# A decoder step on one core: bank copies in the up projection's first pair, and prompt keys kept on chip between two sparse attentions

## What is computed

```python
def swiglu(x, w_gu, w_down):
    gate, up = jnp.split(x @ w_gu, 2, axis=-1)
    return (jax.nn.silu(gate) * up) @ w_down

def indexer_scores(iq, iw, ik):                       # which keys a query may see
    dots = jax.nn.relu(jnp.einsum('bqhd,bsd->bqhs', iq, ik).astype(F32))
    return jnp.einsum('bqhs,bqh->bqs', dots, iw.astype(F32))
# dsa_prompt: per block of 128 queries, scores -> top 256 keys -> softmax(q k^T) v over them
# dsa_sample: the same for 8 queries of a sequence over 2,048 cached keys and 8 new ones
```

## Time and profile before

| | |
|---|---|
| device time, 3 runs | 3459.56, 3460.25, 3463.01 us (median 3460.25) |
| the profiled execution | 3461.72 us, of which the profile's span is 3459.6 us |
| PE busy | 3044.8 us (88%) |
| PEld, DVE, ACT, POOL busy | 2659.6, 1810.4, 1282.3, 748.5 us |
| mean granted TensorE clock | 0.916 of full speed |
| `dsa_sample`, from its first instruction to the next phase's | 601.9 to 824.2 us |
| `dsa_out` | 824.2 to 1241.4 us |
| up projections, first matmul | 1248.6 and (layer 1) about 2639 us |

### The profile page before, as it was taken

One profiled execution on the slowest core, in us unless ns is written; L12 is line 12 of the kernel. 1 busy time (PEld: TensorE's weight loads), 2 busy tenths in 40 slices (PEclk: granted clock), 3 DMA queues, 4 the chain that ended last, 5 costly groups with the idle time before them and its releaser, 6 DMA issues. The chain is left out here.

```text
span 3459.6 us, 55744 instructions
## 1 busy us (share of the span) xinstructions
PE 3044.8 (88%) x21416; PEld 2659.6 (77%) x21435; DVE 1810.4 (52%) x3237; ACT 1282.3 (37%) x2691; POOL 748.5 (22%) x816
## 2 busy tenths in 40 slices
PE   7998887764998869999989988959995999998997
PEld 7798776433565549999989978935664999998997
DVE  2177664794899653433345653414446333333566
ACT  2223453423455343333333432114444333333443
POOL 2100111521111014444300013600001444430002
PEclk8999886885999979999999998959997999999999
DMA  4211003423000012222171102131001222217111
GB/s 128 74 38 33 13 25 89 140 71 140 22 31 25 19 53 82 83 76 75 51 258 38 53 37 56 38 100 59 31 25 49 75 79 79 82 56 253 41 54 52
DMA packets 253548, 240.90 MB, mean 70 GB/s; under 512 B 55874, under 2 KB 213972, under 8 KB 253268
## 3 DMA queue, kind: packets, MB, share of 16 engines
q1 hardware_dynamic: 244548, 217.66, 20.5%
q0 software_dynamic: 8752, 19.81, 1.8%
HBM read 183.25 MB, written 55.89 MB: 69 GB/s over the span
## 5 line engine op out<-in xcount | busy, mean ns | idle before, releaser
L2138 PE MATMUL ffn0u_ps<-ffn0u_x_hi,ffn0u_whi 128*128 128x272 f32 x1232 | 358.9, 291 | 25.7 <-issue 12.0
L2138 PE MATMUL ffn1u_ps<-ffn1u_x_hi,ffn1u_whi 128*128 128x272 f32 x1232 | 358.7, 291 | 25.5 <-issue 12.0
L2138 PE MATMUL ffn1u_ps<-ffn1u_x_hi,ffn1u_wlo 128*128 128x272 f32 x1232 | 356.7, 290 | 0.0
L2138 PE MATMUL ffn0u_ps<-ffn0u_x_hi,ffn0u_wlo 128*128 128x272 f32 x1232 | 356.7, 290 | 0.0
L198 PE MATMUL ine_ps<-ine_w_hi,ine_x_hi 128*128 128x256 f32 (+2 forms) x864 | 264.4, 306 | 5.2 <-DVE ine_w_lo L214 5.0
L2138 PEld LDWEIGHTS ffn0u_ps<-ffn0u_x_hi,ffn0u_whi 128*128 128x128 f32 x1232 | 234.7, 191 | 27.4 <-DVE ffn0u_wlo L2236 14.5
L2138 PEld LDWEIGHTS ffn1u_ps<-ffn1u_x_hi,ffn1u_whi 128*128 128x128 f32 x1232 | 234.7, 191 | 27.2 <-DVE ffn1u_wlo L2236 14.4
L198 PE MATMUL ine_ps<-ine_w_hi,ine_x_lo 128*128 128x256 f32 (+2 forms) x864 | 249.8, 289 | 0.0
L198 PE MATMUL ine_ps<-ine_w_lo,ine_x_hi 128*128 128x256 f32 (+2 forms) x864 | 249.0, 288 | 0.0
L2138 PEld LDWEIGHTS ffn1u_ps<-ffn1u_x_hi,ffn1u_wlo 128*128 128x128 f32 x1232 | 234.9, 191 | 0.0
L2138 PEld LDWEIGHTS ffn0u_ps<-ffn0u_x_hi,ffn0u_wlo 128*128 128x128 f32 x1232 | 234.7, 191 | 0.0
(11 more groups left out here) (513 smaller groups left out, 8411.4 us busy)
## 6 DMA issues: line engine op xcount, KB each, us to landing
aT<-scratch_a SPq DMA_DIRECT2D x44, 544.0 KB, 6.4
ffn0u_raw<-in_ffn_w_gu_dram SPq DMA_DIRECT2D x44, 512.0 KB, 5.2
ffn1u_raw<-in_ffn_w_gu_dram SPq DMA_DIRECT2D x44, 512.0 KB, 5.0
scratch_a<-ffn0u_u SPq DMA_DIRECT2D x44, 272.0 KB, 2.2
scratch_a<-ffn1u_u SPq DMA_DIRECT2D x44, 272.0 KB, 2.3
ffn0d_w<-in_ffn_w_down_dram SPq DMA_DIRECT2D x88, 128.0 KB, 2.5
ffn1d_w<-in_ffn_w_down_dram SPq DMA_DIRECT2D x88, 128.0 KB, 2.5
ine_w<-in_w_in_even_dram SPq DMA_DIRECT2D x5, 1024.0 KB
```

The source lines that it names most:

```text
L2138: last = nc.tensor.matmul(ps[:, bank + h, 0:TOK2], wp, xp, start=(begins and k == 0 and n == 0), stop=(k == KH - 1 and n == 2), skip_group ...
```

## The change

It has two independent parts.

**Up projection (both layers).** For pair 0 only, ACT's two `take` calls (after T2 and after T3) move ahead of the high parts of pair 1's T1 to T4, right behind `gate_one(0)`; DVE's `second_sums(0)` moves ahead of the low parts of pair 1's T1, T2 and T3, right behind those of pair 1's B11 and B21. Pairs 1 to 21 are as before.

**Prompt keys on chip.** `KI`, `KT` and `IKT` become tensors that are allocated ahead of `dsa_sample` and live through `dsa_out`. `dsa_sample` loads the index keys and weights as before into the first 136 columns of the wider `KI`, and, on SP between the pages of sequences 2 and 4, the prompt's keys and values (1 MB, in rows of 1 KB) into the rest. After its last value products PE transposes the keys (8 transposes) and ACT copies them to `KT` (2 copies). `dsa_out` drops the two `KI` loads, 16 transposes and 4 copies, issues the index-query load first and the causal mask second, and its `FIRST` is two entries long. To make room, `diag` in `dsa_sample` becomes a view of `PT`.

```diff
-def dsa_out(nc, st, A, C, O, YTs, hT, bias_ahead):
+def dsa_out(nc, st, A, C, O, YTs, hT, bias_ahead, KI, KT, IKT):
...
-    FIRST = [("index_keys", 0), ("index_keys", 1), ("iq", S0), ("keys", 0), ("keys", 1), ("q", 0)]
+    FIRST = [("iq", S0), ("q", 0)]
...
-                sp.dma_start(causal[:, :], C["causal"]).then_inc(cin, 16)
-
...
-                for f in range(2):
-                    sp.dma_start(KI[:, 4 * f:4 * f + 4, :], st.h_dram[4 * f * P:(4 * f + 4) * P, KI0 - W0:C_DQ - W0].rearrange(
-                        "(i p) c -> p i c", p=P)).then_inc(ki_in, 16)
                 load_iq(S0)
+                sp.dma_start(causal[:, :], C["causal"]).then_inc(cin, 16)
...
-                        f, c0 = u[1], kcol(C_IK if u[0] == "index_keys" else C_DK)
-                        pe.wait_ge(ki_in, 32)
-                        for t in range(4):
-                            last = nc.tensor.transpose(b7[:, t * P:(t + 1) * P], KI[:, 4 * f + t, c0:c0 + P], st.ident[:, :])
...
-                        keys = IKT if u[0] == "index_keys" else KT
-                        nc.scalar.copy(keys[:, 512 * u[1]:512 * (u[1] + 1)], b7).then_inc(p7_read, 1)
...
-def dsa_sample(nc, st, A, C, O, Hs, XT, bias_ahead):
+def dsa_sample(nc, st, A, C, O, Hs, XT, bias_ahead, KI, prompt_KT, IKT):
...
-        spf = PT[:, 0:NP_, :]
+        spf, diag = PT[:, 0:NP_, :], PT[:, NP_:NP_ + 8, :]
...
-                for b in (2, 4, 6):
+                load(sp, 2)
+                sp.dma_start(KI[:, :, W_KI:C_DQ - C_IK], st.h_dram[:, C_DK - W0:C_DQ - W0].rearrange("(t p) c -> p t c", p=P)).then_inc(kv_in, 16)
+                for b in (4, 6):
                     load(sp, b)
+                sp.wait_ge(kv_in, 16)
...
+                pe.wait_ge(kv_in, 16)
+                for f in range(2):
+                    pe.wait_ge(pt_copied, 5 * NP_)
+                    for t in range(4):
+                        last = nc.tensor.transpose(ps[:, 5 + f, t * P:(t + 1) * P], KI[:, 4 * f + t, W_KI:W_KI + P], st.ident[:, :])
+                    last.then_inc(dk_done, 1)
                 pe.wait_ge(y_in, 16)
...
+                for f in range(2):
+                    act.wait_ge(dk_done, f + 1)
+                    nc.scalar.copy(prompt_KT[:, 512 * f:512 * f + 512], ps[:, 5 + f, :]).then_inc(dk_copied, 1)
+                act.wait_ge(dk_copied, 2)
...
                     gate_one(j)
+                    if j == 0:
+                        take(0, S_T2, u2[:, 0, :])
+                        take(0, S_T3, u3[:, 0, :])
                     if more:
                         w_part(j + 1, S_T1)
                         w_part(j + 1, S_T2)
...
-                    take(j, S_T2, u2[:, j % 2, :])
+                    if j >= 1:
+                        take(j, S_T2, u2[:, j % 2, :])
...
-                    take(j, S_T3, u3[:, j % 2, :])
+                    if j >= 1:
+                        take(j, S_T3, u3[:, j % 2, :])
...
                     if j >= 1:
                         first_sums(j)
+                    else:
+                        second_sums(0)
...
-                    second_sums(j)
+                    if j >= 1:
+                        second_sums(j)
```

More of the change, by code:

```diff
@@ L1091, in dsa_out @@
         sem = lambda n: st.sem(f"dsa_{n}")
-        HT, KI = sb("H", [P, RING_T, T_END]), sb("KI", [P, NT, C_DQ - KI0])
-        KT, IKT = sb("KT", [P, SEQ]), sb("IKT", [P, SEQ])
+        HT = sb("H", [P, RING_T, T_END])
         qT, iqT = sb("qT", [P, 2, 4, P]), sb("iqT", [P, 4, P])
@@ L1112, in dsa_out @@
         iq_in = [sem(f"iq_in{k}") for k in range(RING_Q)]
-        h_in, ki_in = [sem(f"h_in{k}") for k in range(RING_T)], sem("keys_in")
+        h_in = [sem(f"h_in{k}") for k in range(RING_T)]
         p7_done, p7_read = sem("pass_done"), sem("pass_read")
@@ L1201, in first_pass @@
                     b7 = first_bank(u)
[L1202 to L1212, removed]
-                    else:
-                        f, c0 = u[1], kcol(C_IK if u[0] == "index_keys" else C_DK)
-                        pe.wait_ge(ki_in, 32)
-                        for t in range(4):
-                            last = nc.tensor.transpose(b7[:, t * P:(t + 1) * P], KI[:, 4 * f + t, c0:c0 + P], st.ident[:, :])
+                    if u[0] == "iq":
+                        T = IQ[:, S0 % RING_Q, :]
+                        pe.wait_ge(iq_in[S0 % RING_Q], 16)
+                    else:
+                        T = tile(0)[:, T_DQ:T_DQ + 512]
+                        wait_tile(pe, 0)
+                    for g in range(4):
+                        last = nc.tensor.transpose(b7[:, g * P:(g + 1) * P], T[:, g * P:(g + 1) * P], st.ident[:, :])
                     last.then_inc(p7_done, 1)
@@ L1372, in first_copy @@
                     act.wait_ge(p7_done, pass_no[u] + 1)
[L1373 to L1378, removed]
-                        keys = IKT if u[0] == "index_keys" else KT
-                        nc.scalar.copy(keys[:, 512 * u[1]:512 * (u[1] + 1)], b7).then_inc(p7_read, 1)
+                    full = first_bank(u).rearrange("p (a t) -> p a t", a=4)
+                    to = iqT[:, :, :] if u[0] == "iq" else qT[:, 0, :, :]
+                    nc.scalar.copy(to, full).then_inc(p7_read, 1)
                 def query_copy(name):
@@ L1493, in add_dots @@
                     if h == 0 and c == 0:
-                        if d == 0:
-                            pool.wait_ge(ki_in, 32)
-                        else:
+                        if d > 0:
                             pool.wait_ge(dot_scaled, d)
@@ L1642, in dsa_sample @@
         pages = sb("pages", [1, NB * PAGES], I32)
-        KI, IQ = sb("KI", [P, NT, W_KI]), sb("IQ", [P, AHEAD, 512])
-        IKT, iqT = sb("IKT", [P, SEQ]), sb("iqT", [P, AHEAD, 4, P])
+        IQ, iqT = sb("IQ", [P, AHEAD, 512]), sb("iqT", [P, AHEAD, 4, P])
         rel, iws = sb("rel", [P, 4, 512]), sb("iws", [P, AHEAD, 8])
         sc, wk, m8 = sb("sc", [P, AHEAD, SEQ]), sb("wk", [P, SEQ]), sb("m8", [P, 8])
-        causal, diag = sb("causal", [P, P]), sb("diag", [P, 8, P])
+        causal = sb("causal", [P, P])
         bias = sb("bias", [P, LH], BF16)
@@ L1673, in dsa_sample @@
         dch, ach = sem("dve_step"), sem("act_step")
-        zeroed = sem("qz_zeroed")
+        zeroed, kv_in, dk_done, dk_copied = sem("qz_zeroed"), sem("prompt_kv_in"), sem("prompt_k_transposed"), sem("prompt_k_copied")
         def key_copy(g):
@@ L1698, in _ @@
                 sp.dma_start(pages[:, :], A["page_table"].rearrange("(o a) b -> o (a b)", o=1)).then_inc(pin, 16)
[L1699 removed]
+                sp.dma_start(KI[:, :, 0:W_KI], st.h_dram[:, C_IK - W0:C_IK - W0 + W_KI].rearrange("(t p) c -> p t c", p=P)).then_inc(ki_in, 16)
                 for a in range(AHEAD):
@@ L3378, in build @@
             bias_ahead = ys.enter_context(nc.sbuf_tensor("bias_ahead", [P, AHEAD, SEQ], BF16, side="right"))
-            dsa_sample(nc, st, A, C, O, Hs, YTs, bias_ahead)
+            KI = ys.enter_context(nc.sbuf_tensor("prompt_KI", [P, NT, C_DQ - C_IK], F32, side="right"))
+            KT, IKT = (ys.enter_context(nc.sbuf_tensor(f"prompt_{n}", [P, SEQ], F32, side="right")) for n in ("KT", "IKT"))
+            dsa_sample(nc, st, A, C, O, Hs, YTs, bias_ahead, KI, KT, IKT)
             st.end_phase()
@@ L3382, in build @@
         hT = hs.enter_context(nc.sbuf_tensor("hT_even", [P, KD, NTOK], F32))
-        dsa_out(nc, st, A, C, O, YTs, hT, bias_ahead)
+        dsa_out(nc, st, A, C, O, YTs, hT, bias_ahead, KI, KT, IKT)
         ys.close()
```

1 line of the change is left out of this document (removed).

## The result

| | before | after |
|---|---|---|
| median of 5 runs | 3460.25 us (3459.56 to 3463.01) | 3442.75 us (3440.77 to 3447.57) |
| the profiled execution, its span | 3461.72, 3459.6 us | 3447.57, 3445.5 us |
| mean granted TensorE clock | 0.916 | 0.920 |

The ratio is 0.995 (95% interval 0.9937 to 0.9964), so the change takes 12 to 22 us off. The forecast was 3444.0, 1.3 us more than the median after.

What follows compares the result with a forecast made beforehand. PE, busy 88% of the span, was taken as the bound, so only its waits pay: 7.9 + 7.4 - 2.8 + 3.8 = 16.3 us off the 3460.25 median gives 3444.0 us, range 3439.0 to 3451.0.

Steps and rivals of the forecast that it cites:

- What PE waited for in pair 0: Up projection: PE's 12.0 us wait ahead of T3 is for ACT's bank copy, queued behind a cast needing POOL.
- The step on `second_sums`: Up projection, pair 0: B22 waits for `second_sums(0)`, now behind only DVE's two low parts, so B22 starts about 1280.1.
- The gain per layer: Up projection: pair 1 starts earlier, by 7.9 us in layer 0 and 7.4 us in layer 1.
- The clock: Ahead of pair 1: about 3.6 us idle slows 14 matmuls, costing 1.4 us per layer, 2.8 together; bounds nothing to 2.1 each.
- POOL is not slowed by `second_sums`: Up projection: the moved `second_sums(0)` on DVE costs POOL's differences nothing, upper bound 0.8 us each.
- The border: Start of `dsa_out`: `dsa_H` lands after 4.5 us, first relu at 833.1 instead of 836.85; gain 3.8 us, bounds 0.6 to 5.1.
- What `dsa_sample` takes on: `dsa_sample`: added transposes, copies and 1 MB load cost nothing; 10.9 us of slack against at most 7.8 of page delay.
- The late tile: Rival, start of `dsa_out`: `dsa_H` takes 7.5 us to land, so the border gains only 0.6; 3447.2 us, chance 0.13.
- the takes were the cause: Rival, up projection, claimed the opposite: PE did not wait for the takes, only the border gains; 3456.4 us, chance 0.04.
- the key load: Rival, SP's queue in `dsa_sample`: the load delays pages past 10.9 us of slack, making the kernel slower; 3469 us, chance 0.02.
- the clock stays down: Rival, up projection: clock at 0.50 through B22 and some 45 matmuls of pair 1, 4.4 us each; 3450.0 us, chance 0.09.
- The sum: Whole kernel: terms add to 16.3 us, giving 3445.4 on the profiled execution and 3444.0 us on the median.

Runs made afterwards that it cites:

- e1_up_only: The kernel before with only the change's up projection edit: median 3447.59 us, ratio 0.9969 to the kernel before.
- e3_takes_only: The changed kernel with DVE's `second_sums(0)` back behind its low parts, ACT's takes left moved: median 3450.05 us, ratio 0.997 to the kernel before.
- e4_gate_ahead: The changed kernel with pair 0's `gate_two` also ahead of ACT's casts, behind the two takes: median 3437.80 us, ratio 0.9933 to the kernel before.
- e5_gate_and_sums: `e4_gate_ahead` with `second_sums(0)` also ahead of DVE's low parts of pair 1's B11 and B21: median 3439.96 us, ratio 0.9932 to the kernel before.
- e8_pair_one: `e5_gate_and_sums` with `third_sums(0)` ahead of DVE's low part of T2 and pair 1's copy after T2 ahead of ACT's casts: 3432.60 us, ratio 0.9911.
- a0_after_again: The changed kernel itself, nothing altered, profiled once more: 3439.08 us in one run, no ratio.

## Why the prediction was right

**What PE waited for in pair 0: right.** The step "a copy that was ready to run at 1271.4 but stood behind a cast that needed POOL" is shown by `e1_up_only`, where nothing but order changed, and the wait ahead of T3 is 0.54 us (0.55 in the changed kernel) where under 1 was forecast. The step on `second_sums` is shown by `e3_takes_only`: without its move 8.2 us of the wait come back at B22.

**The gain per layer: right to 0.1 us in layer 0.** Where the clock held, the gain should be the full 7.9, and the phase became 7.9 shorter (499.8 - 491.9). In layer 1 pair 1 starts 7.6 us earlier in its phase, where 7.4 was forecast. The new wait ahead of pair 1 was to be about 3.6 us and is 3.40, ended by `ffn0u_sg` as forecast. B22 was placed at 1280.1 on the old time axis. The phase begins 0.9 us earlier in the trace after, which makes it 1279.2; it began at 1279.17.

**The clock: right in the mean, too narrow in its bounds.** The step "14 x (0.227 - 0.13) = 1.4 us, off each gain" took a mean for what is one of two outcomes: nothing, or 1.4 to 2.6 us (phases of 493.3 to 494.6 against 491.9). Over the ten starts the mean is 1.3 us, but the upper bound of 2.1 was exceeded in two. In the profiled execution it was 0 and 2.5 us, 2.5 against the forecast 2.8 in sum. That the sum came so near is luck: layer 0 lost nothing, and layer 1 nearly twice the 1.4. The prediction's own sign of being wrong, "a pair 1 at clock 0.50 for more than 3 us", was there in layer 1, with 5.4 us, and in six of the ten starts. The bound from the 22 slow matmuls after 12 us of idle time was no maximum: in the two longest cases pair 1 ran at half clock for 5.4 and 5.5 us, some 24 matmuls of 0.227.

**POOL is not slowed by `second_sums`: right.** 4.84 against 4.77 us, and its instructions took 436 to 444 ns. The rule of the Trainium skill (GPSIMD Engine Reference, "1. Specifications"), that contention comes from DVE instructions with two SBUF inputs or in a two-port mode, agrees with that.

**The border: right.** The landing was put at 4.5 us and took 4.46; the relu at 9 us behind the first DMA, and it came at 8.94. In the other profiles with this code it is 8.2 to 9.4. The term of 3.8 us measured 3.5 in the phase's length of the profiled execution; over all profiles it is 3.1 to 7.1 (410.5 to 414.2 against 417.3 and 417.5), mean 4.8. "A shift of that first relu shifts the phase" holds on average, yet the phase scatters by 4 us behind it, and I had not asked how much a phase does that.

**What `dsa_sample` takes on: right.** 222.3 and 222.3 us, the slack of 10.9 us became 11.8 (743.31 - 731.46).

**The rivals.** The late tile did not come; the takes were the cause; the key load delayed nobody. That the clock stays down was nearest: in seven of ten starts it was at half for 2.9 to 5.5 us of work (13 to 24 matmuls), not through B22 and 45 matmuls; the shorter gaps ahead of T3, T4 and B22 left it at 1.00 in all ten.

**The sum.** It was made against one profiled execution: 16.3 us off 3461.72, 3445.4. Measured there: 16.5 from the three phases, less 2.6 that the input projection took more. Against the medians the change gave 17.5 us.

## What to carry to other kernels

An engine that works off its list in order and has a long wait in it (here casts that wait for GpSimd) holds back everything short that stands behind it, and the profile names such a wait "issue" or by the instruction in front; so look in that engine's timeline for what was ready long before it ran. When one such block is moved, its followers on *every* engine have to move with it: takes alone gave 2.4 us in layer 0, with the sums 7.9, with the gate and the next pair's sums and copy 11.6. Before a term of 2 to 4 us is read off one profile, see how much phases with unchanged code differ between profiles.

## What the runs showed of the hardware

**The same gap, either clock.** PE idle for 3.38 to 3.42 us behind the same work left the clock at 2.4 GHz three times and took it to 1.2 GHz seven times; three of the five executions show both. One thing in the traces goes with it: how long before pair 1's start the clock had last come back, in pair 0. Read in windows of 0.1 us, with the mean clock of the window in which it rose, that is 22.04, 22.05 and 22.31 us in the three starts that kept the clock; in the seven that lost it, it is 20.1 to 22.0 in six (the last 21.96) and 22.36 in one. So it need not be chance. But ten cases, with under 0.1 us between kept and lost at either edge of that range, and no run made for it, do not show a rule. Nor did the clock wait for the gap's end: in layer 1 of the profiled execution it fell at 2666.6, 1.9 us after PE stopped. Without the gap, or with one of 1.5 us (`e4_gate_ahead`), it stayed full.

**The input projection comes in two lengths.** Its code is the same in all twelve profiles. It took 596.3 to 597.5 us in three of them (`e1_up_only`, `e5_gate_and_sums`, `e8_pair_one`) and 601.3 to 604.5 in nine. Windows over it, of `e1_up_only`, then of `a0_after_again`:

```profile
0.00:597.00 597.00, 523.53 (x3801) 454.11 (x3801) 315.70 (x705) 205.21 (x462) 71.87 (x108) 0.90 0.21 57
```

```profile
0.00:601.00 601.00, 529.47 (x3796) 459.41 (x3796) 314.95 (x704) 204.87 (x462) 71.42 (x108) 0.87 0.21 57
```

The same matmuls took 523.5 and 529.5 us of PE at a mean granted clock of 0.90 and 0.87, so the 5 us go with the clock. In the first 596 us of every trace the same 3796 matmul records took 522.3 to 523.7 us in those three profiles and 527.2 to 529.6 in the nine. The difference is as large as a whole term of the change, and may be a good part of the spread between runs of one kernel; for the runs without a profile that is not shown.
